# Two mixtures, attention and a linear tail: down ahead of scatter, fillers, one output piece moved, and a second mixture that splits its pieces in pairs

## The reference

```python
    y = jnp.zeros_like(t)
    for e in range(N_EXPERTS):
        he = jax.nn.silu(t @ w_gate[e]) * (t @ w_up[e])
        y = y + combine[:, e:e + 1] * (he @ w_down[e])
```

## Time and profile before

| | |
|---|---|
| three timed runs | 2337.95, 2346.64 and 2346.89 us, median 2346.64 |
| the profiled execution | 2341.73 us, its span 2339.6 us |
| busy in the span | PE 2216.9 us, DVE 1803.2, ACT 1498.2, POOL 45.4 |
| moved | 593.67 MB, 254 GB/s in the mean |

### The profile page before, as it was taken

One profiled execution on the slowest core, in us unless ns is written; L12 is line 12 of the kernel. 1 busy time (PEld: TensorE's weight loads), 2 busy tenths in 40 slices (PEclk: granted clock), 3 DMA queues, 4 the chain that ended last, 5 costly groups with the idle time before them and its releaser, 6 DMA issues. The chain is left out here.

```text
span 2339.6 us, 35162 instructions
## 1 busy us (share of the span) xinstructions
PE 2216.9 (95%) x12323; PEld 1834.3 (78%) x12323; DVE 1803.2 (77%) x1922; ACT 1498.2 (64%) x1950; POOL 45.4 (2%) x56
## 2 busy tenths in 40 slices
PE   7988799998998999999989899999999999999997
PEld 6877577776776799987767688888888888888886
DVE  5655689987757655566677788989898989898985
ACT  5553488886634543455544587777777777777774
POOL 0000000000003000000003000000000000000000
PEclk9999999999989999999989999999999999999999
DMA  8433199997530354545500698999999999999892
GB/s 316 146 123 130 74 357 372 360 365 265 185 126 2 132 193 177 204 146 190 188 1 33 241 378 335 375 353 355 353 369 347 358 362 355 353 359 375 337 381 77
DMA packets 93734, 593.67 MB, mean 254 GB/s; under 512 B 17312, under 2 KB 20288, under 8 KB 22592
## 3 DMA queue, kind: packets, MB, share of 16 engines
q1 hardware_dynamic: 93632, 592.30, 67.3%
HBM read 591.21 MB, written 1.05 MB: 253 GB/s over the span
## 5 line engine op out<-in xcount | busy, mean ns | idle before, releaser
L426 DVE TENSOR_TENSOR ring_lo<-ring,ring_hi 128x1024 fp32r<-128x1024 f32 (+1 forms) x930 | 1073.4, 1212 | 144.6 <-ACT ring_hi L421 137.9
L421 ACT ACTIVATE ring_hi<-ring 128x1024 fp32r<-128x1024 f32 (+1 forms) x930 | 936.0, 1051 | 178.1 <-PE psum L458 147.7
L456 PE MATMUL psum<-ring_hi,xg_hi 128*128 128x512 f32 x896 | 354.2, 395 | 3.7 <-DVE ring_lo L426 2.4
L458 PE MATMUL psum<-ring_hi,xg_lo 128*128 128x512 f32 x896 | 349.5, 390 | 0.0
L457 PE MATMUL psum<-ring_lo,xg_hi 128*128 128x512 f32 x896 | 348.8, 389 | 0.0
L440 DVE TENSOR_TENSOR ring_lo<-ring,ring_hi 128x2048 fp32r<-128x2048 f32 x95 | 214.7, 2289 | 31.1 <-ACT ring_hi L436 31.0
L456 PE MATMUL psum<-ring_hi,xT_hi 128*128 128x512 f32 (+2 forms) x512 | 199.1, 389 | 14.3 <-DVE ring_lo L426 6.5
L456 PEld LDWEIGHTS psum<-ring_hi,xg_hi 128*128 128x128 f32 x896 | 168.3, 188 | 37.7 <-DVE ring_lo L426 2.9
L458 PEld LDWEIGHTS psum<-ring_hi,xg_lo 128*128 128x128 f32 x896 | 168.1, 188 | 35.8
L458 PE MATMUL psum<-ring_hi,xT_lo 128*128 128x512 f32 (+2 forms) x512 | 195.9, 383 | 0.0
L457 PE MATMUL psum<-ring_lo,xT_hi 128*128 128x512 f32 (+2 forms) x512 | 195.6, 382 | 0.0
(11 more groups left out here) (551 smaller groups left out, 3392.0 us busy)
## 6 DMA issues: line engine op xcount, KB each, us to landing
ring<-in_moe_w_gate_dram SPq DMA_DIRECT2D x112, 1024.0 KB, 7.0
ring<-in_moe_w_up_dram SPq DMA_DIRECT2D x112, 1024.0 KB, 7.5
ring<-in_moe_w_down_dram SPq DMA_DIRECT2D x112, 1024.0 KB, 7.1
ring<-in_w_in_dram SPq DMA_DIRECT2D x38, 1024.0 KB, 5.6
ring<-in_w_gate_dram SPq DMA_DIRECT2D x32, 1024.0 KB, 7.2
ring<-in_w_up_dram SPq DMA_DIRECT2D x32, 1024.0 KB, 7.2
ring<-in_w_down_dram SPq DMA_DIRECT2D x32, 1024.0 KB, 7.2
ring<-in_ffn_w_gate_dram SPq DMA_DIRECT2D x14, 1024.0 KB, 4.8
```

Source lines behind the costliest of these rows:

```text
L421: sc.activation(raw_view(ring_hi, FINE, num, a, width), raw_view(ring, RAW, num, a, width), ACT.Copy) \
L426: v.tensor_tensor(raw_view(ring_lo, FINE, num, a, width), raw_view(ring, RAW, num, a, width), raw_view(ring_hi, FINE, num, a, width).bitca ...
L456: pe.matmul(out_, lhsT[0], rhs[0], start=start, stop=False)
L458: return pe.matmul(out_, lhsT[1], rhs[0], start=False, stop=stop)
```

## The change

1. Second mixture: every pair of gate, up and down pieces is split by one instruction of 2048 columns on ACT and one on DVE, where two of 1024 were. `make_hi_pair` and `make_lo_pair` take the step's number for that; the high part of a pair waits until both pieces of the pair three before are used. At the last, halved, down product two down pieces are split ahead of the hidden values, and two after, where it was three and one.
2. First mixture: `down(i - 1)` stands ahead of the scatter. `copy_output` waits for the scatter that last read its buffer.
3. Second block's attention: 4 fillers at the end of the stage before, once its last outputs are copied, and 4, 3 and 3 ahead of the first three jobs' transposes. In the first block the numbers are given as a tuple, 6, 2, 2, 2, and stay the same.
4. Linear tail: the first output piece's product is done in the linear stage, in two halves ahead of the last two `attended`; the 9 fillers ahead of the last one go. ACT does both silus, each with a table load, in that stage after units 3 and 4. The third and fourth output pieces are split at its end. In the output stage the fifth piece's low part stands ahead of the transposed values' low parts.

```diff
 
-    def make_hi_pair(e, n):
-        e.wait_ge(arrived[n % RAW // 2], 16 * (n // RAW + 1))
-        e.wait_ge(used, n + 2 - FINE)
+    def make_hi_pair(e, n, i=0):
+        e.wait_ge(arrived[n % RAW // 2], i * 16 + 16 * (n // RAW + 1))
+        e.wait_ge(used, count_after((n, i), 2 - FINE))
         sc.activation(pair_view(ring_hi, FINE, n), pair_view(ring, RAW, n), ACT.Copy).then_inc(hi_ready, 2)
 
-    def make_lo_pair(e, n):
-        e.wait_ge(hi_ready, n + 2)
+    def make_lo_pair(e, n, i=0):
+        e.wait_ge(hi_ready, count_after((n, i), 2))
         v.tensor_tensor(pair_view(ring_lo, FINE, n), pair_view(ring, RAW, n), pair_view(ring_hi, FINE, n).bitcast(F32),
...
-    def attend(jobs, busy=0):
+    def attend(jobs, busy=()):
...
-                        if busy:
-                            keep_busy(4, busy if m else 3 * busy)
+                        if m < len(busy):
+                            keep_busy(4, busy[m])
...
             def scalar(e):
                 def body(i, cur, prev, done):
                     if cur:
-                        for k in group.firsts(i):
-                            make_hi(e, group.number(k, i))
+                        for k in group.firsts(i)[::2]:
+                            make_hi_pair(e, *group.number(k, i))
                     if i is None:
                         halves = [slice(c * BANK, (c + 1) * BANK) for c in range(2)]
                         e.wait_ge(gathered, E)
@@ -1312,15 +1312,14 @@
                         e.wait_ge(used, used_before(i))
                         sc.activation(y_hi[:], Y, ACT.Copy).then_inc(y_hi_ok, 1)
                     if cur:
-                        for k in range(4, 8):
-                            make_hi(e, group.number(k, i))
+                        for k in (4, 6):
+                            make_hi_pair(e, *group.number(k, i))
                         e.wait_ge(used, count_after(group.number(3, i)))
                         if prev:
                             e.wait_ge(rows_done, i)
                         sc.activation(s_g[:], bank(0), ACT.Silu).then_inc(silu, 1)
                     if ending(cur, prev):
-                        for k in (8, 9, 10):
-                            make_hi(e, group.number(k, i, cur), 1, 1024)
+                        make_hi_pair(e, *group.number(8, i, cur))
                     if prev:
                         e.wait_ge(hT_t, i)
                         sc.activation(h_hi[:].rearrange("p j s -> p (j s)"), bank(2), ACT.Copy).then_inc(hT_hi, 1)
@@ -1328,8 +1327,8 @@
                         e.wait_ge(ret_t, done + 2)
                         sc.activation(retT[:].rearrange("p h t -> p (h t)"), bank(7)[:, 0:SEQ], ACT.Copy).then_inc(ret_ok, 1)
                     if prev:
-                        for k in range(11 if ending(cur, prev) else 8, 12):
-                            make_hi(e, group.number(k, i, cur), 1, 1024)
+                        for k in (10,) if ending(cur, prev) else (8, 10):
+                            make_hi_pair(e, *group.number(k, i, cur))
                     if gathers(cur):
                         e.wait_ge(used, count_after(group.number(7, i)))
                         e.wait_ge(gathered, cur[0] + 1)
@@ -1346,8 +1345,8 @@
                     elif done is not None and i is not None:
                         make_dispatch(ret, done).then_inc(ret_p, 1)
                     if cur:
-                        for k in group.firsts(i):
-                            make_lo(e, group.number(k, i))
+                        for k in group.firsts(i)[::2]:
+                            make_lo_pair(e, *group.number(k, i))
                     if i is None:
                         halves = [slice(c * BANK, (c + 1) * BANK) for c in range(2)]
                         for c in range(2):
@@ -1366,20 +1365,19 @@
                         e.wait_ge(y_hi_ok, done + 2)
                         v.tensor_tensor(y_lo[:], Y, y_hi[:].bitcast(F32), ALU.subtract).then_inc(y_ok, 1)
                     if cur:
-                        for k in range(4, 8):
-                            make_lo(e, group.number(k, i))
+                        for k in (4, 6):
+                            make_lo_pair(e, *group.number(k, i))
                     if gathers(cur):
                         then_registers(e)
                         make_dispatch(disp, cur[0] + 1).then_inc(next_p, 1)
                     if ending(cur, prev):
-                        for k in (8, 9, 10):
-                            make_lo(e, group.number(k, i, cur), 1, 1024)
+                        make_lo_pair(e, *group.number(8, i, cur))
                     if prev:
                         e.wait_ge(hT_hi, i)
                         v.tensor_tensor(h_lo[:].rearrange("p j s -> p (j s)"), bank(2),
                                         h_hi[:].rearrange("p j s -> p (j s)").bitcast(F32), ALU.subtract).then_inc(hT_lo, 1)
-                        for k in () if ending(cur, prev) else (8, 9):
-                            make_lo(e, group.number(k, i, cur), 1, 1024)
+                        if not ending(cur, prev):
+                            make_lo_pair(e, *group.number(8, i, cur))
                     if done is not None and i is not None:
                         col = slice(done + 1, done + 2) if isinstance(done, int) else bass.ds(done + 1, 1)
                         for h in range(HALVES):
@@ -1390,8 +1388,7 @@
                                                    in1=x[:, h, :], op0=ALU.mult, op1=ALU.add).then_inc(added, 1)
                             e.wait_ge(added, done * 2 + 3 + h)
                     if prev:
-                        for k in (11,) if ending(cur, prev) else (10, 11):
-                            make_lo(e, group.number(k, i, cur), 1, 1024)
+                        make_lo_pair(e, *group.number(10, i, cur))
...
+                    if i:
+                        down(i - 1)
                     if scatter_plan[i]:
                         quarter, experts = scatter_plan[i]
                         e.wait_ge(y_out, 2 * (experts[-1] + 1))
@@ -1590,8 +1589,6 @@
                         if i > 2:
                             e.wait_ge(added, i - 2)
                         scatter(bank(5), quarter, experts, True, True).then_inc(scattered, 1)
-                    if i:
-                        down(i - 1)
...
+                    if 0 < ex < E - 1:
+                        e.wait_ge(scattered, ex)
...
+                        e.wait_ge(free_v.sem, free_v.at(len(chunks) - 1))
+                        e.wait_ge(free_s.sem, free_s.at(len(chunks) - 1))
+                        keep_busy(2, 4)
...
-            attend([cmp0, cmp1, sel1, sel0, win1, win0, diff[2], diff[0], diff[3], diff[1]])
+            attend([cmp0, cmp1, sel1, sel0, win1, win0, diff[2], diff[0], diff[3], diff[1]], busy=(4, 3, 3))
...
+            head = take(4)
+            order = [(c, 2 * half + q) for half in range(2) for c in range(2) for q in range(2)]
+
+            def output_piece(e, p, c, q, parts=range(2)):
+
+                e.wait_ge(lo_ready, p.n + 1)
+                w = [raw_view(r, FINE, (p.n, 0), 2, FF) for r in (ring_hi, ring_lo)]
+                for a in parts:
+                    k = 2 * q + a
+                    for h in range(HALVES):
+                        last = three_passes(bank(2 * c + h), [x_[:, k, h * P:(h + 1) * P] for x_ in xT],
+                                            [w_[:, a, :] for w_ in w], k == 0, k == KT - 1)
+                if parts[-1]:
+                    last.then_inc(used, 1)
...
-                        if m == len(couples) - 1:
-                            e.wait_ge(cross_ok.sem, cross_ok.at(couples[m][0] // 2 + 1))
-                            keep_busy(4, 9)
...
-                    for m in (len(couples) - 2, len(couples) - 1):
+                    e.wait_ge(masked.sem, masked.at(len(couples) - 1))
+                    for a, m in enumerate((len(couples) - 2, len(couples) - 1)):
+                        output_piece(e, head[0], *order[0], range(a, a + 1))
                         attended(m)
                     keep_busy(4, 4)
...
+                        if n == 3:
+                            use_table(SILU)
+                            sc.activation(uc("gog"), uc("gog"), ACT.Silu)
+                        if n == 4:
+                            sc.activation(uc("rog"), uc("rog"), ACT.Silu)
+                            use_table(LOG_EXP)
+                    make_his(e, head[2:])
...
+                    make_los(e, head[2:])
...
-            got = take(KT)
-            order = [(c, 2 * half + q) for half in range(2) for c in range(2) for q in range(2)]
+            got = head + take(KT - 4)
...
                     for i, (p, (c, q)) in enumerate(zip(got, order)):
+                        if i == 0:
+                            continue
                         if i == 4:
                             e.wait_ge(y_lo.sem, y_lo.at(2))
```

(31 more changed lines are left out.)

## The result

The changed kernel takes 2342.58 us in the median of 20 runs (2337.28 to 2344.85), the kernel before 2346.76 in the median of 20 (2337.95 to 2351.72). The ratio is 0.998 with a 95% interval of 0.9972 to 0.9989: 4.2 us faster where 14.5 were forecast.

A forecast was written before the change was run, and what follows sets the result against it. PE was taken to bound the second mixture's steady part, with looser stretches elsewhere. The terms +8.3 - 12 - 4.4 - 6.4 = -14.5 us gave 2327 from the profiled 2341.7 or 2332 from the timed median; 2330 was taken, range 2318 to 2350.

The forecast's parts named there:

- First mixture, -12 forecast: First mixture: down ahead of the scatter shortens eleven full steps by 0.9 us each, plus three shorter scatters: -12 us.
- the new wait for `scattered` ahead of the copy of the outputs: First mixture: next limit after the reordering, a loop through ACT's copy of the outputs, 16.5 us a step against 17.4.
- The doubt about transfers: First mixture: a step of 6.29 MB in 16.5 us wants 382 GB/s where the stretch has 351.
- the bound of -5: First mixture: the gain is only 5 us if the transfers don't follow.
- rival (2): Gains mostly withheld: first mixture gives 5 for want of transfers, clock falls despite attention's fillers; 2345 us, chance 0.23.
- Second mixture, +8.3 forecast: Second mixture: pairs cost nothing in ordinary steps; scatter steps 5, gather 0.2, start 1, end 2.1: +8.3 us, range 3 to 37.
- rival (1): Second mixture: pairs come late in every ordinary step; a shortfall of 0.6 us costs 29: 2359 us, chance 0.12.
- the end, 2.1 forecast: End of the second mixture: the pair 10, 11 is low at 2292.2, PE wants it at 2290.15: +2.1 us.
- the scatter step, 0.7 was forecast: Second mixture: additions to x come 0.8 us later behind the down pair, PE has 0.1 slack: +0.7 each, seven times.
- 1 forecast (0 to 2.4): Start of the second mixture: first pair not split early comes 1.3 us later, a shorter DVE chain offsets: +1 us.
- Attention, -4.4 forecast: Second block's attention: fillers keep the clock, worth 8.1 us, and cost 3.7: -4.4 us; +3.7 if the clock falls.
- Linear tail, -6.4 forecast: Linear tail: one output piece moved a stage earlier and silu waits gone, 3.2 us a layer: -6.4 us, bounds -7 and -3.

The follow-up runs named there:

- e2: The kernel before with the second mixture's pairs of 2048 columns alone: 2361.73 us, ratio 1.0064.
- e3: The kernel before with the first mixture's down product ahead of the scatter, alone: 2342.22 us, ratio 0.9977.
- e5: The kernel before with the fillers of the second block's attention alone: 2336.41 us, ratio 0.9965.
- e6: The kernel before with the changed linear tail alone: 2340.72 us, ratio 0.998.
- e4: e1 with the first mixture's copy of the outputs moved behind the first up pair on ACT, its two successors likewise on DVE: 2321.48 us, ratio 0.9892.
- e1: The changed kernel with the second mixture's pieces split one by one as before, everything else kept: 2328.0 us, ratio to before 0.9916.
- e7: e4 with pairs of 2048 columns for the second mixture's gate and up pieces, down pieces still one by one: 2326.09 us.
- e8: e4 with more fillers in and behind the second block's attention, and DVE's low parts at the linear stage's end made behind POOL's last sums: 2326.51 us.

## Why the prediction was wrong

The direction was right and the size was not: the forecast came to -14.5, the measured difference is -4.2. Measured alone, the parts give +15.4 (e2), -4.1 (e3), -9.0 (e5) and -4.7 (e6), in sum -2.4, which agrees with -4.2 within their intervals. The forecast had +8.3, -12, -4.4 and -6.4. Two errors of 7 to 8 us went one way, one of 5 the other.

**First mixture, -12 forecast, -4.1 measured: the step that failed.** The mechanism was named rightly, "the new wait for `scattered` ahead of the copy of the outputs", and its loop was mis-sized: 16.5 forecast, 17.03 measured. Copy, first high part and hand-over are 3.02 as forecast (417.77 to 420.79). The stretch "from the first low up pair to the second low down pair 7.27" is 7.59 now (420.79 to 428.38). In rows 7 DVE had no pause in it; once ACT's row begins at the scatter's end, silu comes 7.3 us behind the copy's start and DVE waits 0.22 for it. Half of down is 1.97 (430.72 to 432.69) and not 1.82, and the scatter with its signals 2.11, not 2.09. With the last low part's hand-over these make the 0.54 that was missing, 6 us in eleven steps. A loop was added up from durations of a schedule in which it was not the bound, and nearly all of its joints came out longer. The shorter steps ahead of the eleven gave nothing like the 2.3 that I added for them: the whole mixture gained 3.4 us, the eleven steps by 0.37 alone 4.1. The doubt about transfers, which carried the bound of -5 and rival (2), was unfounded (e4).

**Second mixture, +8.3 forecast, +13.6 in the trace, 14.6 and 15.4 by e1 and e2.** Right: the ordinary steps take nothing, although their nearest slack was 0.4 us by the count; rival (1) is out. Right as well: the end, 2.1 forecast and 2.1 measured. Of the scatter step, 0.7 was forecast and 0.7 is what the down pair ahead of the additions costs (19.00 in e7, 19.72 in the changed kernel). What the sum lacked is the gate and up pairs around it, put at 0.03 an expert and measured at 0.4 by e7: 0.1 in the gather step, 0.1 in the step behind it, 0.2 in the scatter step. Together an expert costs 1.14 (from e1's trace to the changed kernel's the distance grows from 5.3 to 13.3 us over seven), where 0.7 was forecast. The start was the largest error: 1 forecast (0 to 2.4), 3.6 and 3.3 in two traces. I counted the first pair's delay of 1.2 and then gave most of it back to a shorter DVE chain. But the second step's first gate pair stands behind a drained pipeline too, and waits 1.1 longer, so that this step begins 2.5 to 2.6 late; it scatters, and its late additions make 0.9 to 1.1 more. The stretch of low clock in it is not what costs: e1, e4 and e8, which split piece by piece, have the same stretch in the same step and lose 0 to 0.2 by it, as e7 does with pairs. (In the kernel before, e3, e5 and e6 the clock does not fall there; what decides it was not looked into.)

**Attention, -4.4 forecast, -8.0 in the trace, -9.0 by e5.** The clock was kept, as forecast. Both sizes were off. From the stages without fillers, 48.0 us with 27.3 of low clock and 38.2 with 3.4, a microsecond at 1.2 GHz costs 0.41, not the 0.33 taken from two close rows. A line through all eight lengths has the same slope, with single stages up to 1.1 us off it. The price of the fillers was set at 1.85 a stage, 0.9 for the four ahead of it and 0.95 for the ten inside. The line gives 36.7 us for a stage that never falls, and the stages with fillers are 37.35, so the ten cost about 0.65 by this estimate. The four stand ahead of the stage's first product, outside these lengths: there the way from the last small product of the stage before to that first product is 3.04 us where it is 2.68 without them, so they cost 0.4. Both lie in waits for the greater part. The Trainium skill's rule ("TensorE: Matmul & The Clock Gate", section Terms) would have 0.5 a microsecond at half the clock, by estimate; this stage is nearer to it than my rows were, and still below. On top of that the trace was one draw of a stage that runs from 38.2 to 48.0 us.

**Linear tail, -6.4 forecast, -4.7 measured.** The output stages gave 3.5 each, 0.2 more than forecast; e6's interval would hold the forecast. The linear stage took back 0.8 where nothing else differed (e1, first layer, with as much low clock in that stage as before): DVE's low parts start 0.3 us behind POOL's last sums and stretch them from 0.96 to 1.85 us. I had dismissed this by an order of events ("when POOL is nearly done"): an overlap of 0.3 us was counted on, it was 0.66 (759.38 to 759.08 + 0.96), and it cost POOL 0.9. e8 shows that taking it away would not have helped, since DVE then ends the stage.

**The two traces.** Clock stretches account for most of what is left. In the changed kernel's trace the stages behind the first layer's attention had 13.7 us of low clock where e1, the same code up to there, had 6.8 and was 2.7 us faster; behind the second layer's it had 13.2 where the kernel before had 10.2; the first gather had one of 3.4 us that cost 1.5 and that stands in neither the kernel before's trace nor in e2's and e5's, but in all the others. The remaining 1.3 us ahead of the first mixture come and go between executions of identical code.

## What to carry to other kernels

Merging two instructions saves engine time and lengthens the latency of the first half. Here it cost nothing where there was slack, and 0.7 to 2.1 us wherever a pipeline started, ended or something else queued behind it: price the drained places, not the steady step. When a reordering takes a wait away, move what the new wait holds back as well: here one instruction placed two microseconds later turned 4 us into about 11. A stage whose clock varies from run to run should be priced from several traces, because one is only a draw.

## What the runs showed that was not expected

- Fillers do more than raise the mean: without them the same attention stage took 38.2 to 48.0 us in eight instances, with them 37.33 to 37.36 in ten.
- More fillers at pauses near the end of the same stage cost 1.3 us a stage (e8) and left the low clock behind the stage at 6.8 us in the first layer and 10.2 in the second, where e4 had 6.8 and 13.7; what sets it was not found.
- Of a stretch of low clock the price depends on what it covers: e4 has one of 3.4 us at the start of the second mixture (1297.88), and that part is as long as before within 0.1 us, since PE's wait of 1.2 us for DVE's additions to x, which the kernel before has in the second step (from 1333.3 to 1334.5), is gone in e4: the slower matmuls ran in time that would have been waited. The same 3.4 us in the first gather, where no such wait follows, cost 1.5.
